# Prompt attention of a hybrid decoder step as one pipeline over all heads, with probabilities turned and scaled by one fp32 product

## The reference

```
q: 1024 x 8 heads x 96      (64 "nope" + 32 rotary columns)
k_nope = lat @ w_uk[:, h]   (1024 x 256 times 256 x 64), 32 rotary columns shared by all heads
v      = lat @ w_uv[:, h]   (64 columns per head)
for each block of 128 queries (t = 0..7):
    s = (q_block @ k.T) / sqrt(96), causal mask, over 128 * (t + 1) keys
    p = softmax(s)
    o_block = p @ v
```

## Time and profile before

| | us |
|---|---|
| median of 3 runs | 1676.03 (1674.02 to 1676.74) |
| the profiled execution, its own time | 1676.3 |
| its span, first to last instruction | 1674.5 |
| mean granted clock of PE | 0.959 |
| PE busy | 1536.4 (92%) |
| DVE, ACT, POOL busy | 720.2, 454.0, 423.8 |
| prompt attention, first scores to last values | 289.9 to 523.4 |

### The profile page before, as it was taken

One profiled execution on the slowest core, in us unless ns is written; L12 is line 12 of the kernel. 1 busy time (PEld: TensorE's weight loads), 2 busy tenths in 40 slices (PEclk: granted clock), 3 DMA queues, 4 the chain that ended last, 5 costly groups with the idle time before them and its releaser, 6 DMA issues.

```text
span 1674.5 us, 23790 instructions
## 1 busy us (share of the span) xinstructions
PE 1536.4 (92%) x9793; PEld 1372.7 (82%) x9793; DVE 720.2 (43%) x1550; ACT 454.0 (27%) x974; POOL 423.8 (25%) x372
## 2 busy tenths in 40 slices
PE   5359967989897999999999999999999999999998
PEld 3159956666665766765999999999999999999997
DVE  2862184665654443444476332323233232323245
ACT  2322043555653333333223202020111102020134
POOL 0420241323322311114120606050421406050300
PEclk9669988999997999999899999999999999999999
DMA  8520113321313444443400303020110202020102
GB/s 304 208 59 1 52 48 110 105 81 62 113 61 143 156 148 170 149 162 114 145 25 1 101 1 101 1 89 13 53 49 15 86 1 88 14 76 26 38 1 107
DMA packets 91530, 137.18 MB, mean 82 GB/s; under 512 B 15867, under 2 KB 65991, under 8 KB 87191
## 3 DMA queue, kind: packets, MB, share of 16 engines
q1 hardware_dynamic: 80431, 85.07, 15.8%
q0 software_dynamic: 7872, 46.14, 7.7%
q10 hardware_dynamic: 3120, 4.46, 0.8%
HBM read 121.98 MB, written 13.79 MB: 81 GB/s over the span
## 4 chain that ended last, share of the span: by engine, by line
PE 82%; DVE 8%; issue 5%; ACT 2%; DMA 1%; POOL 1%; SPq 0%; DVEq 0%; ACTq 0%; POOLq 0%
PE psa L1232 23%; PE psa L1246 22%; PE psa L1210 6%; PE psa L1082 4%; PE psa L1109 4%; PE psa L1149 3%; PE psa L862 3%; PE psa L845 3%; PE psa L427 2%; PE psa L972 2%; PE psa L1112 2%; DVE sqb L407 1%; PE psa L985 1%; PE psa L1000 1%; PE psa L1133 1%
## 5 line engine op out<-in xcount | busy, mean ns | idle before, releaser
L1232 PE MATMUL psa<-hhi,wr 128*128 128x384 f32 (+1 forms) x1536 | 374.5, 326 | 0.0
L1232 PEld LDWEIGHTS psa<-hhi,wr 128*128 128x128 f32 x1536 | 270.9, 188 | 0.1
L1246 PE MATMUL psa<-g_hi,wd_hi 128*128 128x384 f32 (+1 forms) x768 | 251.2, 327 | 0.0
L1232 PE MATMUL psa<-hlo,wr 128*128 128x384 f32 (+1 forms) x768 | 250.3, 326 | 0.0
L1246 PE MATMUL psa<-g_hi,wd_lo 128*128 128x384 f32 (+1 forms) x768 | 250.2, 326 | 0.0
L1246 PE MATMUL psa<-g_lo,wd_hi 128*128 128x384 f32 (+1 forms) x768 | 250.2, 326 | 0.0
L1629 ACT ACTIVATE g_relu<-psa 128x384 f32<-128x384 f32 (+1 forms) x96 | 45.5, 474 | 600.9 <-PE psa L1232 600.9
L2038 DVE SCALAR_TENSOR_TENSOR xT<-psa,modT,xT 128x384 f32<-128x384 f32 (+1 forms) x216 | 123.1, 571 | 191.7 <-PE psa L1246 160.9
L607 POOL TENSOR_SCALAR wr<-wraw 128x1024 fp32r<-128x1024 f32 x34 | 36.5, 1074 | 571.1 <-PE psa L1232 492.1
L2103 DVE TENSOR_TENSOR psa<-psa,g_relu 128x384 f32<-128x384 f32 (+1 forms) x96 | 52.2, 544 | 261.0 <-ACT g_relu L1629 261.0
L1232 PEld LDWEIGHTS psa<-hlo,wr 128*128 128x128 f32 x768 | 144.1, 188 | 0.1
(11 more groups left out here) (334 smaller groups left out, 2713.8 us busy)
## 6 DMA issues: line engine op xcount, KB each, us to landing
wmod<-in_w_mod SPq DMA_DIRECT2D x8, 2048.0 KB, 7.9
wraw<-in_w_up SPq DMA_DIRECT2D x32, 512.0 KB, 4.1
wraw<-in_w_down SPq DMA_DIRECT2D x32, 512.0 KB, 3.4
wmod<-in_w_mod POOLq DMA_DIRECT2D x4, 2048.0 KB, 13.5
x_scr<-xT SPq DMA_DIRECT2D x1, 4352.0 KB, 19.5
xstage<-in_x_prompt SPq DMA_DIRECT2D x8, 512.0 KB, 8.8
wraw<-in_w_out SPq DMA_DIRECT2D x8, 512.0 KB, 6.2
out_y_p<-yst SPq DMA_DIRECT2D x8, 512.0 KB, 2.6
```

The lines of the kernel that those rows point to most:

```text
L1232: mm = pe.matmul(out[:, :N], w[:, c * P:c * P + P], x[:, c, c0:c0 + N], start=(c == 0 and q == 0), stop=(c == KD - 1 and q == 2))
L1246: mm = pe.matmul(out[:, :N], w[:, c, n * P:n * P + P], x[:, c, c0:c0 + N], start=(c == 0 and q == 0), stop=(c == FG - 1 and q == 2))
```

## The change

Only the prompt attention is changed. The loop over heads becomes one loop over 64 blocks (i = 8 hh + t), and per head:

- `prob` has three buffers. POOL no longer multiplies the block: it makes `diag` = identity times `rden`, 128x128, one buffer, once the block before has been turned. `turn` is now an fp32 product of the prob tile (weights) with `diag`: it transposes and scales.
- The turned probabilities are kept in fp32, unsplit (`pt0`, `pt1`): each group is read once, four of twelve by ACT, eight by DVE. `values` is an fp32 product with `v_all` itself, 64 columns of weights; even tiles go to rows 0-63 of bank 2, odd ones to rows 64-127. `vhl` and its splitting on POOL are gone.
- `qT` and `kT` have two buffers; the next head's `turn_q` comes in steps t = 1, 2 and its `make_k` in t = 3, 4, each half through bank 3 in turn. The modulation uses bank 3 too, in t = 5, 6, 7, as 2, 3 and 3 matmuls instead of four pairs. The second values of a head come in t = 0, 1 of the next.
- The scale of the softmax is folded into the queries, and the negated maximum is one instruction.
- SP's order is: modulation load of head hh (when the head before has done its modulation's matmuls, t = 7), then directly the queries and `wuk_raw` of head hh + 1.

```diff
-            g.tensor_scalar(prob[:, t % 2, :n], prob[:, t % 2, :n], rden[:, t % 2:t % 2 + 1], 1.0,
-                            ALU.mult, ALU.mult).then_inc(sem("p_ready"), 1)
+        for i in range(NT):
+            hh, t = i // PT, i % PT
+            g.wait_ge(sem("rden"), i + 1)
+            if i >= 1:
+                g.wait_ge(sem("pt_mm"), groups_turned(i - 1))
+            g.tensor_scalar(diag[:, :], ident[:, :], rden[:, i % 4:i % 4 + 1], 1.0, ALU.mult, ALU.mult)\
+             .then_inc(sem("p_ready"), 1)
+            if t == 0 and hh + 1 < H:
+                split_wuk(hh + 1)
...
-                    mm = pe.transpose(bank(PT_BANKS[group % 3])[:, (j - j0) * P:(j - j0) * P + P],
-                                      prob[:, t % 2, j * P:j * P + P], ident[:, :])
+                    mm = pe.matmul(out[:, (j - j0) * P:(j - j0) * P + P], prob[:, i % 3, j * P:j * P + P], diag[:, :],
+                                   start=True, stop=True)
...
-                for q, x in enumerate((ptb_hi, ptb_lo)):
-                    mm = pe.matmul(bank(2 + w)[:, c0:], vhl[:, u, j, :], x[:, j, c0:],
-                                   start=(j == 0 and q == 0), stop=(j == 4 * w + 3 and q == 1))
+                c0 = max(0, j - 4 * w) * P if j > 1 else 0
+                rows = slice(DV * (j % 2), DV * (j % 2) + DV)
+                mm = pe.matmul(bank(2)[rows, c0:], v_all[:, j, hh * DV:hh * DV + DV], x[:, j, c0:],
+                               start=(j < 2), stop=(j >= 4 * w + 2))
...
+        for i in range(NT):
+            hh, t = i // PT, i % PT
+            if t == 0 and hh >= 1:
+                mods_back(hh - 1)
+                values(hh - 1, 1, range(4))
+            if t == 1 and hh >= 1:
+                values(hh - 1, 1, range(4, 8))
+            if t in (1, 2) and hh + 1 < H:
+                turn_q(hh + 1, t - 1)
+            if t in (3, 4) and hh + 1 < H:
+                make_k(hh + 1, t - 3)
+            if t == 5:
+                values(hh, 0, range(4))
+                mods(hh, (0, 1))
+            if t == 6:
+                mods(hh, (2, 3, 4))
+            if t == 7:
+                mods(hh, (5, 6, 7))
+            if i + 2 < NT:
+                scores(i + 2)
+            turn(i)
...
         sp.wait_ge(sem("kr_lo"), 1)
-        for i in range(H // 2 - 1):
-            heads(i, False)
-        heads(H // 2 - 1, True)
+        mods_in(0)
+        for hh in range(1, H):
+            head_in(hh)
+            mods_in(hh)
```

More of the change, by code:

```diff
@@ L936, in _ @@
         barrier(pe, 2)
[L939 to L962, removed]
@@ L964, in scores, with turn_q @@
-        def scores(hh, t):
-            pe.wait_ge(sem("exp"), 8 * hh + t + 1)
+        def turn_q(hh, w):
+            out = bank(3)
+            if w == 0:
+                pe.wait_ge(sem("qh_in"), 16 * hh + 16)
+            if hh == 0:
+                out = bank(3 - w)
+            elif w == 0:
+                pe.wait_ge(sem("mod_ev"), 3 + hh)
+            else:
+                pe.wait_ge(sem("q_lo"), 2 * hh + 1)
+            for t in range(4):
+                mm = pe.transpose(out[0:DQ, t * P:t * P + P], qh[:, 4 * w + t, :], ident[:, :])
+            mm.then_inc(sem("q_turned"), 1)
@@ new lines, in make_k @@
+        def make_k(hh, w):
+            out = bank(3)
+            if w == 0:
+                pe.wait_ge(sem("wuk_split"), hh + 1)
+            if hh == 0:
+                out = bank(w)
+            elif w == 0:
+                pe.wait_ge(sem("q_lo"), 2 * hh + 2)
+            else:
+                pe.wait_ge(sem("k_lo"), 2 * hh + 1)
+            for c in range(CC):
+                for q, (a, x) in enumerate(products(wuk_hi, wuk_lo, latT_hi, latT_lo)):
+                    mm = pe.matmul(out[0:DN, :], a[:, c, :], x[:, c, 512 * w:512 * w + 512],
+                                   start=(c == 0 and q == 0), stop=(c == CC - 1 and q == 2))
+            mm.then_inc(sem("k_mm"), 1)
@@ L1002, in values @@
             if j == 4 * w + 3:
                 mm.then_inc(sem("pv_mm"), 1)
[L1005 to L1013, removed]
-                pe.wait_ge(sem("wmod2_in"), 16 * hh + 16)
[L1015 to L1031, removed]
-                mod_turn(pe, modrow[:, 0, :], bank(2)).then_inc(sem("mod_turned"), 1)
-                values(hh, u, 1, range(4))
-                if not (last and u):
-                    first_scores(hh + 1)
-                values(hh, u, 1, range(4, 8))
@@ L1038, in _, with mods @@
-        turn_q(0)
-        make_k(0)
-        first_scores(0)
-        for i in range(H // 2 - 1):
-            heads(i, False)
-        heads(H // 2 - 1, True)
+        def mods(hh, chunks):
+            if chunks[0] == 0:
+                pe.wait_ge(sem("wmod2_in"), 16 * hh + 16)
+                if hh + 1 < H:
+                    pe.wait_ge(sem("k_lo"), 2 * hh + 4)
+                else:
+                    pe.wait_ge(sem("mod_ev"), 4 + hh)
+            mm = mod_matmuls(pe, wmod2, bank(3), chunks)
+            if chunks[-1] == KD - 1:
+                mm.then_inc(sem("mod_mm"), 1)
@@ new lines, in mods_back @@
+        def mods_back(hh):
+            pe.wait_ge(sem("mod_row"), hh + 5)
+            mod_turn(pe, modrow[:, 0, :], bank(3)).then_inc(sem("mod_turned"), 1)
+        for w in range(2):
+            turn_q(0, w)
+        for w in range(2):
+            make_k(0, w)
+        pe.wait_ge(sem("kr_lo"), 1)
+        scores(0)
+        scores(1)
+        for i in range(NT):
+            hh, t = i // PT, i % PT
+            if t == 0 and hh >= 1:
[17 more added lines that the diff above has]
+            turn(i)
@@ L1044, in _ @@
+        mods_back(H - 1)
+        values(H - 1, 1, range(8))
         barrier(pe, 3)
@@ L1906, in _, with mods_in, maximum @@
[L1906 to L1912 removed]
+        def mods_in(hh):
+            v.wait_ge(sem("mod_turned"), hh + 5)
+            modulate(16 + 4 * hh, bank(3)).then_inc(sem("mod_ev"), 1)
+        def maximum(i):
+            n = (i % PT + 1) * P
+            v.wait_ge(sem("s_mm"), i + 1)
+            if i >= 4:
+                v.wait_ge(sem("exp"), i - 3)
+            v.reduce_max(nmx[:, i % 4:i % 4 + 1], psa[:, 2048 + 1024 * (i % 2):2048 + 1024 * (i % 2) + n], axis=AX_X, negate=True)\
+             .then_inc(sem("neg"), 1)
@@ new lines, in _ @@
+        for w in range(2):
+            q_lo(0, w)
+        for w in range(2):
+            k_lo(0, w)
+        maximum(0)
+        maximum(1)
+        one_over_sum(0)
+        for i in range(NT):
+            hh, t = i // PT, i % PT
+            if i >= 1:
+                the_rest(i - 1)
+            if t == 0 and hh >= 1:
+                mods_in(hh - 1)
+            if t == 1 and hh >= 1:
+                out_sum(hh - 1, 1)
+            if t in (1, 2) and hh + 1 < H:
+                q_lo(hh + 1, t - 1)
+            if t in (3, 4) and hh + 1 < H:
+                k_lo(hh + 1, t - 3)
+            if t == 5:
+                out_sum(hh, 0)
+            if i + 1 < NT:
+                one_over_sum(i + 1)
+            if i + 2 < NT:
+                maximum(i + 2)
```

356 lines of the change are left out of this document (155 added, 201 removed).

## The result

| | before | after |
|---|---|---|
| median, us | 1676.18 (4 runs) | 1702.82 (4 runs, 1697.41 to 1705.6) |
| the profiled execution, us | 1676.3 | 1701.77 |
| its span, us | 1674.5 | 1699.6 |
| mean granted clock of PE | 0.959 | 0.964 |
| PE busy, us | 1536.4 | 1571.2 |

The ratio is 1.0151, with a 95% interval from 1.0127 to 1.0175. The forecast was 1696, range 1679 to 1708. DVE, ACT and POOL have less to do, as the change's text leads one to expect, and PE has 35 us more.

What follows compares the result with a forecast made beforehand. PE bounds the kernel, with 82% of the chain of waits. Per head 30.0 work + 0.7 bank 3 + 1.9 for `qh` = 32.6 us; stage end 543.3 for 523.4, so 1676.3 + 20 = 1696, range 1679 to 1708.

Steps and rivals of the forecast that it cites:

- The tile: Turning by diagonal product: 0.22 us a tile against a transposition's 0.11, 36 tiles, 4.0 us more per head.
- The base of 24.9: PE's work in a head before the change: 28.55 us less idle times of 0.4, 3.0 and 0.2.
- Values: fp32 products in pairs: equal to before within 0.1 us, plus 0.2 per head for entering the two-column-half mode.
- Modulation: Four pairs become a pair and two triples, each triple's third costing a pair's 0.87 us: +0.9 per head.
- Bank 3: Waits for ACT's and DVE's copies between halves of the next head's queries: 0.7 us per head, bounds 0 and 3.
- `qh` behind the 2 MB: Queries land 9.1 us after the modulation load's issue; `turn_q` waits 1.9 us per head, 3.5 in head 0.
- rival C: The new wait for `qh` lowers the clock: 1.6 us seven times, 11, giving 1707; chance 0.17 with longer bank 3 waits.
- The waits that go: PE's stalls of 3.0 and 0.4 us per head vanish, and the 1.3 on average that the clock takes.
- A: Rival: a tile as cheap as a transposition, 0.11 us; 21.7 less, 1675; chance 0.19 including combinations with B and E.
- B: Rival: the queue serves both loads side by side, `qh` not held by the 2 MB; 13 us less, 1683; chance 0.14.
- D: Rival: weight loads and streams in turn, 0.44 us a tile; 63 us more, 1759; chance 0.02.
- E: Rival: modulation triples run as one and a half pairs; 7 us less, 1689; chance 0.48 together with the main forecast.

Runs made afterwards that it cites:

- E5: Kernel before with the product alone: POOL writes the diagonal of reciprocals, PE turns and scales by fp32 product; 1688.72 us, ratio 1.0063.
- E3: E2 with POOL scaling the probabilities in their block and plain transpositions instead of products with the diagonal; 1659.11 us, ratio 0.9894.
- E2: E1 with the modulation's matmuls as 2, 2 and 4 instead of 2, 3 and 3; 1682.74 us, ratio 1.0029.
- E1: Changed kernel with the next head's queries and key weights issued ahead of the modulation's 2 MB; 1684.75 us, ratio 1.0051.
- E4: Changed kernel with plain transpositions; POOL still writes the unread diagonal, division by the row sums left out; 1682.65 us, ratio 1.0037.
- E6: E3 with four of the modulation's matmuls at t = 6 and two at t = 7; 1652.34 us, ratio 0.9849.
- E7: E6 with the next head's queries turned and copied in t = 0, 1 instead of t = 1, 2; 1648.68 us, ratio 0.9831.
- E8: Kernel before with POOL scaling only the first 128 probabilities of each block, the rest unscaled; 1666.87 us, ratio 0.9946.

## Why the prediction was right, and where its 6 us are

The direction and the mechanism hold at every main step. The stage's end is 8 us later than forecast (551.3 for 543.3); that the total is only 6 off is in part luck, since some 3 us come back afterwards by the clock of the next stage, which the forecast did not have. Per head the forecast was 30.0 of work + 0.7 at bank 3 + 1.9 for `qh` = 32.6. What came is 31.1 + 0.2 + 1.9 + 0.3 = 33.5. The 31.1 is read so: take from each of the four heads at a clock of 1.00 its wait for `qh`, as 34.02 - 2.70 and 32.66 - 1.34, and each leaves 31.3, 0.2 of it bank 3's.

For the first point below, two rows from after and two from E5: a turning, and the keys' first product behind it.

```profile
401.45 1.11 PE L984 MATMUL psa<-diag,prob 128*128 128x128 f32 x8
402.31 0.47 PE L945 MATMUL psa<-latT_hi,wuk_hi 128*64 128x512 f32 x1
```

```profile
407.40 1.95 PE L986 MATMUL psa<-diag,prob 128*128 128x128 f32 x16
409.11 0.47 PE L961 MATMUL psa<-latT_hi,wuk_hi 128*64 128x512 f32 x1
```

- *The tile.* 0.22 was taken, and one more tile in a row does cost that: eight take 386.01 - 384.08 = 1.93, seven 381.75 - 380.04 = 1.71. But 7 x 0.22 is 1.54: there is 0.17 on top, where seven transpositions pay 0.05 (397.90 to 398.72, 0.82). This is not a price of each turning. It comes where an fp32 product follows the turning, as the modulation's, the values' or the queries' do (0.12 to 0.17 in the head shown). Four tiles with the keys' fp32r products (one record each) behind them pay nothing (402.31 - 401.45 = 0.86), and so do eight in E5 (409.11 - 407.40 = 1.71). Over a head, adding up the times from each row's start to the next row's start, turning takes 9.05 us after and 4.13 before: 4.9 more and not 4.0. **This is the term that was mis-sized**, 0.9 per head and 7 us over eight. In E5, with other neighbours, it is 4.2. E3 against E2 confirms that the product is the main cost.
- *The base of 24.9.* The prediction took 3.6 us of idle time off the head before; PE's recorded waits in it are 2.86 and 0.35, which leaves 25.3. Counted alike, then, the work grew by 5.8 for 5.1 forecast, and the other 0.4 of the 1.1 between 31.1 and 30.0 lies in the base. (In the earlier trace rows the eight records of 512 columns are four products; 0.885 a pair is right.)
- *The Trainium skill's rule* (page "TensorE: Matmul & The Clock Gate", Part 3, The mechanism) would have made a tile 0.44, loads and streams in turn. The records contradict it here: 0.22 for two loads of 128x128 and two streams. The same section also lets a load into a background weight buffer overlap; the rows agree with that, and do not show which buffer was used.
- *Values.* Two pairs of 512 columns and an entry of the two-column-half mode were put at 1.77 + 0.1; the rows show 388.87 - 387.00 = 1.87. Over the head they take 4.8 against 4.5, start to start: 0.3 more, the 0.1 and the entries of the mode together.
- *Modulation.* A triple of 1.81 against 1.74; E2 shows that it costs what two pairs do. Predicted +0.9 per head, start to start 4.59 against 3.93: +0.7.
- *Bank 3.* Predicted 0.7 per head, measured 1.3 us in four waits: 0.2. In E1, without the wait for `qh` ahead of it, it is 0.6; that this wait gives ACT and DVE time to catch up is the likely reason, and was not tried.
- *`qh` behind the 2 MB.* Predicted 3.5 in head 0 and 1.9 after; measured 3.10, then 1.34, 1.73, 2.70, 1.26, 2.47, 1.80, 1.9 on average. The landing was put at 9.1 to 9.3 us after the modulation's load; the turnings that it releases start 9.0 to 10.5 us after. E1 shows the cause by removing it: 18 us.
- *The clock*, rival C. In two later heads it was 0.95, and each cost 0.9 us: 34.70 - 2.47 = 32.2 for 31.3. In head 0 it was 0.84, and 0.88 in E1, without that wait. The sum had nothing for it: 0.3 per head on average. Rival C priced it at 1.6 in seven heads; it came at 0.9 in two, and head 0 lost 0.3 more than its wait against E1's. Six periods of E1 are 13.0 us shorter. The waits for `qh` (11.3) and the clock (1.9) are 13.2 of that, but E1 waits 2.1 more at bank 3, so some 2 us of the 13.0 stand in no named term; 1.4 of them are PE time between rows that no wait is named for (a head's work, start to start, is 30.99 after and 30.76 in E1).
- *The waits that go* went: no wait for POOL is left on PE's list, and the weight loads waited for `diag` 1.9 us in all, hidden.
- *Rivals.* A needed 0.11 a tile: refuted by the rows. E4 measured 20 for its 21.7, but that nearness is chance: the clock took back what the waits were to take. B needed `qh` unheld: refuted by the landing; E1 is B made true, 1685 against its 1683. D and E are refuted by 0.22 and 1.81.

So the expected gain was there. Against the kernel before, the pipeline saves 3.4 us of stall and 1.3 of clock per head, less 0.2 to 0.6 at bank 3; the product gives back 4.9, the triples 0.7, the load order 2.2 with its clock. E1 to E3 take the last three back one by one, and what then remains is faster than before by 1%; the two reorderings of E6 and E7 make it 1.7%.

Open: why the granted clock fell after the waits of 2.47 and 1.80 and not after the one of 2.70, why a turning pays more ahead of an fp32 product, and why the next stage started at a higher clock.

## What to carry to other kernels

When PE carries the chain, an idea that hands DVE's, ACT's or POOL's work to PE must be priced on PE alone: 0.14 us more for each of 288 tiles was 39 us of PE work and 24 us net, and nothing in the time shows the 30, 22 and 46 us that DVE, ACT and POOL saved. Order the small load that somebody waits for ahead of the large one that nobody needs yet; both were in the same loop, and swapping them was two thirds of the loss. And do one part at a time: the pipeline was a gain hidden under a loss, and the matmuls that depend on nothing belong ahead of whatever waits last.

## What the runs showed of the hardware

- A fall of the clock is not set by the length of the wait alone. With nearly the same work in a head, PE's stall of 2.6 to 2.9 us was followed by a clock of 0.94 in four of six heads (before), 2.0 to 2.2 us in two of six (E8), and up to 1.5 us in none (E5, with the product's added work); in the later heads of the changed kernel 2.47 and 1.80 were followed by one, 2.70 was not; in E4 all waits (2.3 to 3.4) were. Each cost 1.6 us in the kernel before and in E8, 0.9 in the changed one, and by estimate 1.2 to 3.1 in E4, where the same wait of 2.32 was followed by 0.94 once and 0.89 once. The counts are of one execution of each kernel.
- In a run of fp32 products of 128x128 weights with 128 columns each further one costs 0.22 us, in a run of transpositions 0.11. What a run costs on top goes by what follows it: 0.17 for eight products ahead of the fp32 products of L438, nothing for eight (E5) or four ahead of fp32r products.
- PE work that falls ahead of a result that another engine is still making is covered by the stall: in E5 the six tiles ahead of it take 0.67 us longer, POOL's instruction 0.64 less (0.375 for 1.015), and the wait went from 2.86 to 1.48. With what the clock gave back, 33 us of work cost 11 of time.
